# Keys of two MLA heads in one product, a new order at the change of layers and at the start, and a wait for GpSimd, in a two-layer hybrid attention kernel

## The chip, the cores and the metric

One core of one Trainium2 chip runs the whole program. The metric is the device time of one execution in microseconds; lower is better. "Span" is the time between the first and the last instruction that the profiler saw.

## The reference

Two layers over 256 context tokens and 512 latent tokens of width 1024, in float32. Each layer modulates a layer norm with shift and scale from `w_ada`, projects to 2784 columns and attends in three head groups. Only the MLA group is shown: its keys and values come from one product with `w_ukv`, in which each head has 64 key columns followed by 64 value columns.

```python
def mla_kv(zckv, zkr, g, w_ukv, tabs):
    kv = (rms_norm(zckv, g) @ w_ukv).reshape(B, L, MLA_HEADS, MLA_NOPE + MLA_V)
    k_nope, v = jnp.split(kv, [MLA_NOPE], axis=-1)
    ...
def hybrid_layer(...):
    sh_l, sc_l, gt_l = jnp.split(jax.nn.silu(c) @ p["w_ada"] + p["b_ada"], 3, axis=-1)
    hl = layer_norm(xl) * (1 + sc_l[:, None, :]) + sh_l[:, None, :]
    ... = jnp.split(hl @ p["w_in"], IN_SPLITS, axis=-1)
    ...
    y_l = merge_groups(o_a, o_b, o_m, ga_l, gb_l, gc_l, p["w_out"])
    xl_new = layer_norm(DEEPNORM_ALPHA * xl + gt_l[:, None, :] * y_l, p["ln_g"], p["ln_b"])
```

## The kernel before

Tokens lie in six tiles of 128 (tiles 0 and 1 are context, 2 to 5 latent). Every large product is done as three products on values split in a high and a low part (`three`, lines 982 to 984); ScalarE writes the high part of a weight slice (line 1515), GpSimd the low part (line 1899). The engines' programs are written out by hand, each in its own order, and meet only in semaphores; the SyncE queue issues all loads in its own order. So an instruction that waits holds all that is behind it on its engine.

Start (layer 0). Loads: tiles 0 to 3 of the input, the shift part of quarter 0 of `w_ada` (1 MB), tiles 4 and 5, its scale part, then weight pieces and quarters in turn. VectorE takes row statistics (`rows_in`), GpSimd the root, VectorE or ScalarE scales the rows (`scale_rows`), TensorE turns each tile (`turn_x`, line 1043), ScalarE copies it back (`put_back`). TensorE forms a quarter's modulation rows (`ada_half`, line 1009), VectorE copies them, TensorE turns and adds strips by a product with `pick` (`turn_quarter`, line 1024), VectorE adds the bias (`quarter_columns`), ScalarE modulates, VectorE splits, and `project` begins. Quarters 1 to 3 are turned between products of the first chunk.

Attention. 20 units in ten pairs per layer; units 14 to 19 are the six MLA heads, pairs 7 to 9. Pair p's scores, exponents (ScalarE, line 1627), partial sums (GpSimd, `sum_probs`, line 1954; last one VectorE, `sum_last`, line 2218) and value products overlap with the row maxima of the pairs behind it (`max_tile` on TensorE, line 1225; `reduce_max` on VectorE, line 2183). Products go through a ring of three PSUM banks in the order of the list `RING`. In pairs 4, 5 and 6 `mla_head` (line 1177) makes q and k of the units of the pair three further on: the even unit before scores 4, the odd one after scores 5. `mla_copy` takes them out of the ring on ScalarE, `mla_rope` turns q on VectorE, and a pair later `mla_high` (ScalarE) and `mla_low` (VectorE) split them. Today one "k" part has 128 stationary columns of one head, of which `mla_copy` keeps rows 0 to 63. Eight probability buffers are used in turn, so an exponent waits for the sums that read its buffer.

Change of layers. `project_out` ends with the second half of the output product, one tile after another in the order 2, 3, 4, 5, 0, 1 ("tile n" below and in the prediction counts in this order, from 0). Per tile VectorE does `gained_tile` (residual, centring, gain) and `new_row`; ScalarE squares twice (`square_rows`, line 1768), GpSimd takes roots (`row_root`), ScalarE writes the normalised row (`next_row`, line 1777), TensorE turns it, ScalarE modulates (`modulate_next`, line 1791), VectorE splits it (`split_next`, lines 2392 and 2393), and TensorE starts layer 1's first chunk with the slices that are ready: three of the ring (`NW`) and three held aside (`HELD`, slices 3 to 5) in buffers that the output product still reads, so that they are split at its end. Line 336 and line 274:

```python
def mla_parts(L):
    return [("q", 1), ("k", 1)] + ([("q", 0)] if L < DEPTH - 1 else []) + [("k", 0)]
HELD = [("in", 1, CHUNK_ORDER[0], k) for k in (3, 4, 5)]
```

## Time and profile before

| | us |
|---|---|
| median of 3 runs (lowest, highest) | 968.3 (966.56, 972.94) |
| the profiled execution | 967.27 |
| its span | 965.5 |
| TensorE busy | 923.2 |
| VectorE / GpSimd / ScalarE busy | 565.5 / 511.2 / 430.2 |

Busy times are unions of the instructions of an engine over the span. PE is TensorE, PEld its weight loads, DVE VectorE, ACT ScalarE, POOL GpSimd, SPq the SyncE queue. The start of the next product, not the duration of one, tells what a product costs, since they overlap in the pipeline. The granted clock is 1.00 at 2.4 GHz and 0.50 at 1.2 GHz.

### The profile page before, as it was taken

The page shows a single profiled execution, that of the slowest core. Times are in us where ns is not written, and L with a number is a line of the kernel's source. Part 1 is how long each engine was busy: PE and PEld are TensorE (multiplying, and loading weights), DVE is VectorE, ACT ScalarE, POOL GpSimd, SP SyncE. Part 2 cuts the span into 40 slices and gives each one's busy share as a digit, 9 for nine tenths or more (in the row PEclk, how much of TensorE's full clock was granted, in tenths as well). Part 3 has the DMA queues.
Part 4 walks back from the last instruction along what each step waited for, and adds up shares of the span by engine and source line. Part 5 has one row for each costly group of instructions (what it writes and reads, how often), then busy time and mean ns, then how long its engine had stood idle before and what let it go on. Part 6 is the DMA issues. An engine that isn't in the chain of part 4 may idle for free.

```text
span 965.5 us, 13483 instructions
## 1 busy us (share of the span) xinstructions
PE 923.2 (96%) x4699; PEld 665.4 (69%) x4699; DVE 565.5 (59%) x900; ACT 430.2 (45%) x877; POOL 511.2 (53%) x431
## 2 busy tenths in 40 slices
PE   5999999999999999999999799999999999999996
PEld 4678667889655665665678589888984555565684
DVE  5469133513687669962228838667257757884346
ACT  5331221413565466655234852235344545664432
POOL 3137223324687645565546517455438875466672
PEclk9999999999999999999999999999999999999998
DMA  9957672214533200020453202322352311020252
GB/s 321 279 209 242 217 244 78 76 39 100 133 70 80 50 17 18 18 66 1 146 177 113 81 16 77 87 81 82 83 121 63 71 46 25 9 74 10 85 178 88
DMA packets 51754, 95.85 MB, mean 99 GB/s; under 512 B 9508, under 2 KB 24720, under 8 KB 50664
## 3 DMA queue, kind: packets, MB, share of 16 engines
q1 hardware_dynamic: 51688, 94.99, 32.4%
q8 instruction: 39, 0.64, 0.3%
q14 instruction: 27, 0.22, 0.1%
HBM read 71.32 MB, written 4.21 MB: 78 GB/s over the span
## 4 chain that ended last, share of the span: by engine, by line
PE 83%; DVE 9%; ACT 4%; POOL 2%; issue 2%; DMA 0%; POOLq 0%; SPq 0%; ACTq 0%; DVEq 0%
PE banks L982 15%; PE banks L984 14%; PE banks L983 14%; PE banks L1250 12%; PE banks L1272 11%; PE banks L1225 6%; PE banks L993 2%; PE banks L1291 2%; PE banks L1284 1%; DVE negmax L2183 1%; DVE area_b L2352 1%; PE banks L1123 1%; PE banks L1387 1%; DVE scr L2349 1%; ACT late_bias L1768 1%
## 5 line engine op out<-in xcount | busy, mean ns | idle before, releaser
L1899 POOL TENSOR_TENSOR w_split<-w_raw,w_split 128x512 fp32r<-128x512 f32 (+4 forms) x121 | 147.7, 1230 | 224.4 <-ACT w_split L1515 224.4
L982 PE MATMUL banks<-w_split,area_a 128*128 128x512 f32 (+3 forms) x606 | 230.5, 380 | 9.0 <-DVE area_a L2393 6.8
L984 PE MATMUL banks<-w_split,area_a 128*128 128x512 f32 (+3 forms) x606 | 223.0, 368 | 0.0
L983 PE MATMUL banks<-w_split,area_a 128*128 128x512 f32 (+3 forms) x606 | 222.4, 367 | 0.0
L2183 DVE TENSOR_REDUCE negmax<-banks 128x1 f32<-128x768 f32 x160 | 149.2, 952 | 80.1 <-PE banks L1225 79.7
L1515 ACT ACTIVATE w_split<-w_raw 128x512 fp32r<-128x512 f32 (+4 forms) x121 | 68.5, 580 | 192.2 <-PE banks L984 185.4
L1627 ACT ACTIVATE area_z<-banks 128x512 f32<-128x512 f32 x196 | 108.8, 598 | 80.0 <-PE banks L1250 76.6
L982 PEld LDWEIGHTS banks<-w_split,area_a 128*128 128x128 f32 x606 | 114.5, 189 | 41.0 <-issue 19.1
L1250 PE MATMUL banks<-area_a 97*128 97x512 f32 (+4 forms) x448 | 129.0, 399 | 4.4 <-ACT area_z L1627 3.1
L984 PEld LDWEIGHTS banks<-w_split,area_a 128*128 128x128 f32 x606 | 114.5, 189 | 16.7
L983 PEld LDWEIGHTS banks<-w_split,area_a 128*128 128x128 f32 x606 | 114.8, 189 | 12.8
L1250 PEld LDWEIGHTS banks<-area_a 97*128 97x128 f32 (+2 forms) x448 | 77.2, 190 | 57.3 <-issue 23.9
L1272 PE MATMUL banks<-area_z,vals 128*64 128x512 f32 x360 | 92.5, 618 | 0.0
L1954 POOL TENSOR_TENSOR area_b<-area_b,area_z 128x512 f32<-128x512 f32 x56 | 74.0, 1344 | 19.0 <-ACT area_z L1627 19.0
L1225 PE MATMUL banks<-area_a 96*128 96x384 f32 (+1 forms) x288 | 77.2, 357 | 5.2 <-DVE negmax L2183 3.7
L1225 PEld LDWEIGHTS banks<-area_a 96*128 96x128 f32 (+1 forms) x288 | 49.7, 191 | 31.9 <-issue 25.1
L1954 POOL TENSOR_TENSOR w_raw<-w_raw,area_z 128x512 f32<-128x512 f32 x38 | 49.2, 1322 | 6.4 <-ACT area_z L1627 6.4
L2156 DVE COPY area_b<-banks 128x512 f32<-128x512 f32 (+1 forms) x27 | 15.7, 583 | 61.9 <-PE banks L1123 61.9
L1935 POOL TENSOR_TENSOR area_g<-area_g,o_v 128x768 f32<-128x768 f32 (+3 forms) x20 | 26.4, 1319 | 47.4 <-DVE o_v L2244 31.6
L1272 PEld LDWEIGHTS banks<-area_z,vals 128*64 128x64 f32 x360 | 21.4, 138 | 34.0 <-issue 24.4
L1515 ACT ACTIVATE area_b<-banks 128x512 f32<-128x512 f32 (+4 forms) x66 | 31.9, 510 | 28.6 <-PE banks L984 25.4
L1627 ACT ACTIVATE late_bias<-banks 128x512 f32<-128x512 f32 x64 | 35.5, 596 | 18.1 <-PE banks L1250 15.2
(224 smaller groups left out, 1475.0 us busy)
## 6 DMA issues: line engine op xcount, KB each, us to landing
w_raw<-in_w_in_dram SPq DMA_DIRECT2D x32, 512.0 KB, 4.6
area_g<-in_w_ada_dram SPq DMA_DIRECT2D x13, 1024.0 KB, 6.3
area_g<-in_w_ada_dram SPq DMA_DIRECT2D x16, 512.0 KB, 4.8
w_raw<-in_w_out_dram SPq DMA_DIRECT2D x16, 512.0 KB, 4.5
area_a<-parts SPq DMA_DIRECT2D x72, 96.0 KB, 2.2
area_a<-parts SPq DMA_DIRECT2D x30, 192.0 KB, 3.6
area_b<-in_x_dram SPq DMA_DIRECT2D x8, 512.0 KB, 7.4
w_raw<-in_w_in_dram SPq DMA_DIRECT2D x8, 352.0 KB, 3.3
```

The costliest lines, as they stand in the source:

```text
L982: nc.tensor.matmul(dst, a[0], b[0], start=first, stop=False)
L983: nc.tensor.matmul(dst, a[0], b[1], start=False, stop=False)
L984: return nc.tensor.matmul(dst, a[1], b[0], start=False, stop=last)
L1225: mm = nc.tensor.matmul(banks[:, b0 + j, 0:384], f[0][0:rows, t * P:(t + 1) * P], f[2][0:rows, j * 384:(j + 1) * 384], start=True, stop=True)
L1250: mm = nc.tensor.matmul(dst[:, at:at + cols.stop - cols.start], f[kf][0:rows, kt * P:(kt + 1) * P], f[qf][0:rows, cols], start=(i == 0), s ...
L1272: mm = nc.tensor.matmul(banks[64 * u:64 * u + 64, 3, :], vals[:, step, value_head(2 * p + u), :], prob(L, p, step, u), start=(step == 0), ...
L1515: return nc.scalar.activation(dst, src, ACT.Copy)
L1627: nc.scalar.activation(prob(L, p, step, u), banks[:, r % NRING, :], ACT.Exp, scale=SCALE[pair_family(p)]).then_inc(p_ready, 1)
L1899: op = nc.gpsimd.tensor_tensor(lo, raw, hi.bitcast(F32), ALU.subtract)
L1935: nc.gpsimd.tensor_tensor(g, g, o, ALU.mult).then_inc(gated, 1)
L1954: nc.gpsimd.tensor_tensor(total(L, p, u), first, prob(L, p, step, u), ALU.add).then_inc(pool_summed, 1)
L2183: nc.vector.tensor_reduce(negmax[:, p % 2, at:at + 1], banks[:, b0:b0 + 2, 0:384], AX.XY, ALU.max, negate=True).then_inc(max_read, 1)
```

## The change

MLA keys: an even unit has only its "q" parts; an odd unit's "k" parts use 128 stationary columns that hold the keys of both heads of the pair, and `mla_copy` copies rows 0 to 63 to the even unit's buffer and 64 to 127 to the odd one's. For that the split `ukv` is laid out with all keys first and all values behind. Change of layers: two slices are held (3 and 4), in `ukv` and in the free end of `parts`, which are free after the last scores; ScalarE and GpSimd split them around the first tile; slice 5 goes through the ring. The orders of ScalarE and VectorE for the last tiles are rewritten. GpSimd waits at the first sums of pair 1 for VectorE's last sums of pair 0. Start: tile 4 is loaded ahead of quarter 0; TensorE's and VectorE's orders are changed; a quarter is turned with four transposes, and VectorE sums the strips. Hunks that only pass the unit to `mla_parts` are left out, and leading context with them.

```diff
@@ -271,7 +271,7 @@
-HELD = [("in", 1, CHUNK_ORDER[0], k) for k in (3, 4, 5)]
+HELD = [("in", 1, CHUNK_ORDER[0], k) for k in (3, 4)]
@@ -333,9 +333,12 @@
-def mla_parts(L):
-
-    return [("q", 1), ("k", 1)] + ([("q", 0)] if L < DEPTH - 1 else []) + [("k", 0)]
+def mla_parts(L, u):
+
+    groups = (1, 0) if L < DEPTH - 1 else (1,)
+    if u % 2 == 0:
+        return [("q", g) for g in groups]
+    return [("q", 1), ("k", 1)] + [("q", g) for g in groups[1:]] + [("k", 0)]
@@ -376,13 +379,13 @@
-            RING += [("mla", _L, 2 * _p + 6, part) for part in mla_parts(_L)]
+            RING += [("mla", _L, 2 * _p + 6, part) for part in mla_parts(_L, 2 * _p + 6)]
         if now:
             RING += [("s", _L, _p, s, u) for s in (4, 5) for u in range(2)]
         if not last:
             RING += [("rows", _L, 1)]
         if head_pair(_p + 3):
-            RING += [("mla", _L, 2 * _p + 7, part) for part in mla_parts(_L)]
+            RING += [("mla", _L, 2 * _p + 7, part) for part in mla_parts(_L, 2 * _p + 7)]
@@ -757,10 +760,9 @@
-            for t in range(4):
+            for t in range(5):
                 load_x(t)
             load_quarter(0, 0)
-            load_x(4)
@@ -931,6 +933,12 @@
+        def held_slice(k):
+
+            flat = (ukv if k == 3 else parts)[:].rearrange("p a n -> p (a n)")
+            at = 0 if k == 3 else 2048
+            return [flat[:, at + i * 512:at + (i + 1) * 512] for i in range(2)]
+
@@ -939,7 +947,7 @@
-                hi, lo = late_slice(k - 3)
+                hi, lo = held_slice(k)
@@ -947,7 +955,9 @@
-                return [(flat[:, 0:768], ukv[:, 0, :], ukv[:, 1, :])]
+                src = flat[:, 0:768].rearrange("p (h z n) -> p z h n", h=6, z=2)
+                hi, lo = (ukv[:, i, :].rearrange("p (z h n) -> p z h n", z=2, h=6) for i in range(2))
+                return [(src[:, z], hi[:, z], lo[:, z]) for z in range(2)]
@@ -962,13 +972,13 @@
-                eng.wait_ge(filled, USE["y", s[1] - 1, 1, out_tiles(s[1] - 1)[-1]] + 1)
+                scored(eng, s[1] - 1, NPAIR - 1)
             elif s[0] in ("in", "out"):
                 slice_used(eng, s)
             if s[0] == "uq":
                 eng.wait_ge(filled, USE["z", s[1], LAST, TILES - 1] + 1)
             if s[0] == "out" and s[2] == 0 and s[3] < NW:
-                eng.wait_ge(ring_filled, N_RINGB["mla", s[1], NUNIT - 1, mla_parts(s[1])[-1]])
+                eng.wait_ge(ring_filled, N_RINGB["mla", s[1], NUNIT - 1, mla_parts(s[1], NUNIT - 1)[-1]])
@@ -1018,11 +1028,8 @@
-                for i in range(2):
-                    for w in range(2):
-                        at = w * 256 + i * P
-                        mm = nc.tensor.matmul(banks[:, 6, 4 * i + 2 * w:4 * i + 2 * w + 2], ada_rows[:, q % 2, at:at + P],
-                                              pick[:], start=True, stop=True)
+                for b in range(4):
+                    mm = nc.tensor.transpose(banks[:, 6, b * P:(b + 1) * P], ada_rows[:, q % 2, b * P:(b + 1) * P], ident[:])
@@ -1138,7 +1145,7 @@
-                v = [ukv[:, i, :].rearrange("p (h n) -> p h n", h=6)[:, :, 64:128] for i in range(2)]
+                v = [ukv[:, i, 384:768] for i in range(2)]
@@ -1186,7 +1193,7 @@
-                        mm = three(dst, [ukv[:, i, h * P:(h + 1) * P] for i in range(2)],
+                        mm = three(dst, [ukv[:, i, (h - 1) * 64:(h + 1) * 64] for i in range(2)],
@@ -1494,12 +1501,13 @@
-                    for t in range(4):
+                    for t in range(3):
                         turn_x(L, t)
                     ada_half(0, 0)
+                    turn_x(L, 3)
                     turn_x(L, 4)
+                    ada_half(0, 1)
                     turn_x(L, 5)
-                    ada_half(0, 1)
@@ -1579,17 +1587,23 @@
-                for part in mla_parts(L):
+                for part in mla_parts(L, u):
                     r = N_RINGB["mla", L, u, part] - 1
                     what, g = part
-                    rows = P if what == "q" else 64
+                    src = banks[:, r % NRING, 0:len(GROUPS[g]) * P]
                     act.wait_ge(ring_filled, r + 1)
-                    copy(qk_t[0:rows, 2 * (m % 2) + (what == "k"), tokens(g)],
-                         banks[0:rows, r % NRING, 0:len(GROUPS[g]) * P]).then_inc(ring_free, 1)
+                    if what == "q":
+                        op = copy(qk_t[:, 2 * (m % 2), tokens(g)], src)
+                    else:
+                        copy(qk_t[0:64, 2 * ((m - 1) % 2) + 1, tokens(g)], src[0:64])
+                        op = copy(qk_t[0:64, 2 * (m % 2) + 1, tokens(g)], src[64:128])
+                    op.then_inc(ring_free, 1)
             def mla_high(L, u):
                 m = N_MLA[L, u]
                 act.wait_ge(mla_roped, m)
+                if u % 2 == 0:
+                    act.wait_ge(ring_free, N_RING_FREE["mla", L, u + 1, mla_parts(L, u + 1)[-1]])
@@ -1815,23 +1829,24 @@
+                split_w(HELD[0])
                 square_rows("new", L, ts[0])
-                for n in range(1, len(ts)):
+                split_w(HELD[1])
+                for n in range(1, len(ts) - 1):
                     square_rows("next", L, ts[n - 1])
-                    if n == len(ts) - 1:
-                        for s in HELD:
-                            split_w(s)
                     square_rows("new", L, ts[n])
-                    if n == len(ts) - 1:
-                        next_row(L, ts[n - 1])
                     if n >= 3:
                         modulate_next(L + 1, ts[n - 3])
-                    if n < len(ts) - 1:
-                        next_row(L, ts[n - 1])
-                square_rows("next", L, ts[-1])
-                next_row(L, ts[-1])
-                for t in ts[-LAG:]:
-                    modulate_next(L + 1, t)
+                    next_row(L, ts[n - 1])
+                square_rows("next", L, ts[4])
+                modulate_next(L + 1, ts[2])
+                square_rows("new", L, ts[5])
+                next_row(L, ts[4])
+                modulate_next(L + 1, ts[3])
+                square_rows("next", L, ts[5])
+                modulate_next(L + 1, ts[4])
+                next_row(L, ts[5])
+                modulate_next(L + 1, ts[5])
@@ -1945,6 +1960,7 @@
+                        pool.wait_ge(dve_summed, N_DVE_SUM[L, 0, 1])
@@ -2035,11 +2051,10 @@
-                        if n == len(ts) - 1:
+                        row_root("new", L, ts[n])
+                        if n == 0:
                             split_w(HELD[0])
                             split_w(HELD[1])
-                        row_root("new", L, ts[n])
-                    split_w(HELD[2])
@@ -2406,11 +2421,15 @@
+                    if n == 5:
+                        split_next(ts[1])
                     gained_tile(n, t)
-                    if n > LAG:
-                        split_next(ts[n - LAG - 1])
+                    if n == 4:
+                        split_next(ts[0])
+                    elif n == 5:
+                        split_next(ts[2])
                     new_row(n, t)
-                for t in ts[-LAG - 1:]:
+                for t in ts[3:]:
@@ -2433,11 +2452,12 @@
-                col = ada_col[:, 0].rearrange("p (w k) s -> p k w s", w=2)[:, 2 * q:2 * q + 2]
-                sums = banks[:, 6, 0:8].rearrange("p (k w s) -> p k w s", k=2, w=2)
-                bias = bias_col[:].rearrange("p (w k) -> p k w", w=2)[:, 2 * q:2 * q + 2]
-                nc.vector.tensor_tensor(col, sums, bias.unsqueeze(3).broadcast_to((P, 2, 2, 2)),
-                                        ALU.add).then_inc(quarter_ready, 1)
+                strips = banks[:, 6, :].rearrange("p (b j r) -> p b r j", b=4, j=4)[:, :, 0:2, :]
+                chain(nc.vector.tensor_reduce(strip_sum[:], strips, AX.X, ALU.add))
+                col = ada_col[:, 0].rearrange("p (w k) s -> p w k s", w=2)[:, :, 2 * q:2 * q + 2]
+                bias = bias_col[:].rearrange("p (w k) -> p w k", w=2)[:, :, 2 * q:2 * q + 2]
+                nc.vector.tensor_tensor(col, strip_sum[:].rearrange("p (w k) s -> p w k s", w=2),
+                                        bias.unsqueeze(3).broadcast_to((P, 2, 2, 2)), ALU.add).then_inc(quarter_ready, 1)
@@ -2472,14 +2492,12 @@
-                    dve.wait_ge(pool_const, 1)
-                    nc.vector.tensor_reduce(pick[:], ident[:].rearrange("p (j r) -> p r j", j=4)[:, 0:2, :], AX.X, ALU.add)
                     rows_in(1)
                     rows_in(2)
                     scale_rows(1)
                     rows_in(3)
+                    rows_in(4)
                     scale_rows(3)
-                    rows_in(4)
```

## Rows read from the trace of the kernel before

**Rows 1.** The page: busy time, share of the span and instructions of TensorE
```profile
PE 923.2 (96%) x4699; PEld 665.4 (69%) x4699; DVE 565.5 (59%) x900; ACT 430.2 (45%) x877; POOL 511.2 (53%) x431
```

**Rows 2.** Waits of TensorE in the whole span: line, releaser, total, times, longest
```profile
PE banks L982 <- DVE area_a L2393: 6.8, 1, 6.8
...
PE banks L1291 <- DVE w_raw L2218: 1.0, 2, 0.7
```

**Rows 3.** Timeline, layer 1, pairs 5 and 6: start, duration, instruction, [idle before]
```profile
820.31 0.40 PE L982 MATMUL banks<-cmp_t,ukv 128*128 128x512 f32 x1
...
821.01 0.28 PE L982 MATMUL banks<-cmp_t,ukv 128*128 128x256 f32 x1
...
821.36 0.99 PE L1250 MATMUL banks<-area_a 97*128 97x512 f32 x2
...
822.74 1.82 DVE L2183 TENSOR_REDUCE negmax<-banks 128x1 f32<-128x768 f32 x2 [2.29 <-PE banks L1225]
...
828.99 1.08 ACT L1627 ACTIVATE area_z<-banks 128x512 f32<-128x512 f32 x2 [2.48 <-PE banks L1250]
```

**Rows 4.** Stretch of layer 0's pair 6: busy us of PE, PEld, DVE, ACT, POOL; clock
```profile
381.00:404.00 23.00, 22.47 (x115) 14.57 (x116) 21.02 (x26) 13.86 (x39) 14.72 (x11) 1.00 0.08 18
```

**Rows 5.** Line 1515 (ScalarE copies) from 330 to 420: ns min/median/max, forms
```profile
L1515 ACT ACTIVATE area_b<-banks x24: 378/490/601, 339.4 to 397.2; 128x512 f32<-128x512 f32 x6, 64x512 f32<-64x512 f32 x6, 128x256 f32<-128x256 f32 x6, 64x256 f32<-64x256 f32 x6
```

**Rows 6.** Timelines of VectorE, ScalarE, GpSimd and TensorE, change of layers
```profile
542.91 1.23 DVE L2393 TENSOR_TENSOR area_a<-area_z,area_a 128x1024 fp32r<-128x1024 f32 x1
...
546.65 0.69 DVE L2349 TENSOR_TENSOR scr<-banks,area_g 128x512 f32<-128x512 f32 x1
...
548.37 1.28 DVE L2373 SCALAR_TENSOR_TENSOR o_t<-area_b,row_mean,area_g 128x1024 f32<-128x1024 f32 x1
...
551.51 2.17 DVE L2393 TENSOR_TENSOR area_a<-area_z,area_a 128x1024 fp32r<-128x1024 f32 x1
...
542.82 2.88 ACT L1791 ACTIVATE area_z<-banks,ada_col 128x128 f32<-128x128 f32 x8
...
546.70 1.17 ACT L1768 ACTIVATE late_bias<-area_b,row_mean 128x1024 f32<-128x1024 f32 x1
...
549.66 2.94 POOL L1899 TENSOR_TENSOR cmp_t<-w_raw,cmp_t 128x512 fp32r<-128x512 f32 x2
...
553.73 0.79 PE L982 MATMUL banks<-w_split,area_a 128*128 128x512 f32 x1 [6.81 <-DVE area_a L2393]
```

**Rows 7.** Stretches with the granted clock (after the five busy times)
```profile
554.00:556.00 2.00, 2.00 (x5) 1.55 (x6) 1.60 (x1) 0.57 (x2) 1.61 (x2) 0.50 0.00 0
...
558.00:560.00 2.00, 2.00 (x12) 1.86 (x11) 0.88 (x1) 0.30 (x3) 1.42 (x3) 0.77 0.08 28
...
28.00:32.00 4.00, 4.00 (x38) 1.90 (x38) 0.90 (x2) 0.40 (x1) 1.27 (x1) 0.77 1.10 349
```

**Rows 8.** Timeline of the start
```profile
6.18 1.86 SPq L743 DMA_DIRECT2D area_g<-in_w_ada_dram  x1
...
14.80 1.28 DVE L2059 BATCH_NORM_STATS2 stats<-area_b 128x6 f32<-128x512 f32 x2
...
20.56 1.17 ACT L1515 ACTIVATE w_split<-w_raw 128x512 fp32r<-128x512 f32 x2
...
20.75 1.07 PE L1009 MATMUL banks<-area_g,c_silu 128*32 128x256 f32 x16
...
23.99 2.51 ACT L1544 ACTIVATE area_b<-area_b,ada_col 128x256 f32<-128x256 f32 x4 [1.29 <-DVE ada_col L2439]
```

**Rows 9.** DMA issues from 6 to 6.5: KB each, us to landing
```profile
area_g<-in_w_ada_dram SPq DMA_DIRECT2D x1, 1024.0 KB, 12.8
```

**Rows 10.** Timeline: a quarter turned today (x8) and four plain transposes (x4)
```profile
33.31 0.95 PE L1024 MATMUL banks<-pick,o_t 128*128 128x2 f32 x8
...
294.09 0.60 PE L1302 MATMUL banks<-ident,scr 128*128 128x128 f32 x4
```

**Rows 11.** Timeline, layer 1: VectorE's last sums of pair 0
```profile
734.95 4.23 DVE L2218 TENSOR_TENSOR w_raw<-w_raw,late_bias 128x512 f32<-128x512 f32 x2
```

More of the change, by code:

```diff
@@ L460, in hybrid_layers @@
         bias_col = sb("bias_col", [P, 16])
-        pick = sb("pick", [P, 2])
+        strip_sum = sb("strip_sum", [P, 4, 2])
         stats = sb("stats", [P, TILES, 2, 6])
@@ L642, in operands_free @@
             elif u == 19:
-                eng.wait_ge(ring_filled, N_RINGB["mla", L, 19, mla_parts(L)[-1]])
+                eng.wait_ge(ring_filled, N_RINGB["mla", L, 19, mla_parts(L, 19)[-1]])
             else:
@@ L1581, in mla_copy @@
                     act.wait_ge(split_lo, N_SPLIT[L, "gqa2"])
-                for part in mla_parts(L):
+                for part in mla_parts(L, u):
                     r = N_RINGB["mla", L, u, part] - 1
                     what, g = part
-                    rows = P if what == "q" else 64
+                    src = banks[:, r % NRING, 0:len(GROUPS[g]) * P]
                     act.wait_ge(ring_filled, r + 1)
-                    copy(qk_t[0:rows, 2 * (m % 2) + (what == "k"), tokens(g)],
-                         banks[0:rows, r % NRING, 0:len(GROUPS[g]) * P]).then_inc(ring_free, 1)
+                    if what == "q":
[4 more added lines that the diff above has]
+                    op.then_inc(ring_free, 1)
             def mla_high(L, u):
```

2 lines of the change are left out of this document (1 added, 1 removed).

## The prediction

> **What bounds the kernel now.** I read four views in this order. The page first: TensorE is busy for 923.2 us of a span of 965.5 [rows 1], and no other engine comes near, so time falls only where TensorE gets less to do or stands less. The reader is to see how little standing there is to win: 42 us in all. The waits of TensorE say where [rows 2]: one wait of 6.8 us for VectorE's split of a tile (line 2393, the change of layers) is by far the longest, and two for the last sums (line 2218) make 1.0 us. Then the timeline around the edited places, and the granted clock of the stretches: after the long wait TensorE runs at half rate for some 5 us [rows 7]. The profiled execution took 967.27 us (span 965.5 and 1.8 around it); the median of the runs shown is 968.3, 1.0 above. I make the sum on 967.27 and add that 1.0 at the end.
>
> **Keys of two heads in one product.** Today `mla_head` uses 128 stationary columns of one head, 64 key columns and 64 value columns that `mla_copy` throws away. Afterwards two heads' keys fill the 128, on odd units only; for units 14, 16, 18 in each layer the two "k" parts vanish. One pair of parts is three products of 512 columns and three of 256: 820.31 to 821.36, that is 1.05 us [rows 3]. Six units: 6.3 us of pure TensorE work. Is it on the path? Behind the even unit's products, VectorE stood 2.29 us at 822.74 until TensorE's next maximum tile [rows 3]; so there the saving goes straight through. Against it: in one of the four pairs in which VectorE also splits MLA operands (`mla_low`; p = 5 and 6 of both layers) it is busy 21.02 of 23.00 us [rows 4], TensorE 22.47. The 1.98 us that VectorE has free exceed 1.05, but not all lie in the right place. I take 1.05 in the two pairs p = 4 and 0.85 in the other four: 2.1 + 3.4 = **5.5**; bounds 2.1 (nothing in the four) and 6.3. ScalarE's copies stay equal in number but move: an odd unit has two more, 0.60 and about 0.38 us, since 64 and 128 rows cost the same [rows 5]. Queued behind them is the next pair's first exponent, before which ScalarE stands 2.48 us today [rows 3]: hidden, at most 0. What they cost if that cover goes is the last rival. The even unit's rope waits only for "q" now, earlier than before; `mla_high` of the even unit waits for copies that ScalarE has already done in its own order. The `ukv` split in two instructions each on ScalarE and GpSimd adds a start-up or two where both idle: 0. The ring has two slots fewer at an even unit; the slots then needed (the row maxima, the outputs) are freed long before: 0.
>
> **Change of layers.** (Tiles are counted here in the order in which the output product makes them, 0 to 5.) Today TensorE starts tile 1 at 553.73, 6.81 us after the end of tile 0's products [rows 6]. VectorE first does `gained_tile` for tile 5 (from 546.65 until the instruction begun at 548.37 ends at 549.65), then the split of tile 1, whose second half takes 2.17 us instead of the 1.23 of tile 0's, because GpSimd splits held slices from 549.66 [rows 6]. The new order: the split of tile 1 stands ahead of `gained_tile` of tile 5; its input is ready (ScalarE modulates it from 542.82 for 2.88 us [rows 6]). So it runs 546.65 to about 548.6 without GpSimd beside it (some 0.7 for the copy and 1.23). The held slices are split some 25 us earlier, in a buffer free since the last scores; what they delay is VectorE's chain for tile 0, which is serial from there on and never waits for TensorE. I charge 1.0, one VectorE instruction lengthened as above (2.17 - 1.23 = 0.94); bounds 0 and 1.9 (two). Tile 1 is thus ready at 549.6 and TensorE waits 2.9 us. What is late next: turning tile 5 needs `next_row`(5), which stands on ScalarE behind the square of tile 5 and the modulation of tile 4. Walking the lists with 1.2 for a square (546.70 [rows 6]) and as much for a row, 2.9 for a modulation and 1.9 for a split gives 562.6 for it, while TensorE arrives 2.5 us sooner. Two waits, 5.4 us. Today's loss is 6.8 plus the low clock: 0.50 granted in 554 to 556 and 0.77 in 558 to 560 [rows 7], so low until about 558.9, 5.2 us at half rate, 2.6 lost; 9.4. Difference 4.0. A clock that falls in the first wait is mostly absorbed by the second; I keep 0.5 for it: **3.5**, bounds 0 (both waits with a full low stretch, and VectorE delayed by 1.9) and 6. Slice 5, no longer held, goes into the slot of slice 0, free when the last tile has used it: 12 products of 0.23 us (820.31 to 821.01 for three [rows 3]) are 2.8 us of cover for one ScalarE and one GpSimd split (0.6, and 1.5 as in the 2.94 for two [rows 6]): 0. Its piece stays longer in the raw buffer, and the SyncE queue waits there before a load wanted tens of us later: 0.
>
> **The lock between VectorE and GpSimd.** The row shows 0.94 us for one VectorE instruction beside GpSimd's split [rows 6]. The Trainium skill, "SBUF — State Buffer", Who interferes with whom, says more: whoever comes first holds the shared ports for its whole instruction and the other is fully blocked. By that rule two GpSimd splits of 1.47 us each (2.94 for two [rows 6]) could cost the chain 2.9 instead of my 1.0, and the sum would be 1.9 us smaller. It speaks against the early split; the last sums below show a blocking of that size, so I keep it in the range.
>
> **Start.** The tile-4 row statistics begin at 14.80 [rows 8] because tile 4's load is queued behind the first 1 MB of weights; moved ahead of it they follow tile 3's at about 13.3. Tile 5's load keeps its place, behind the same bytes. The second half of quarter 0 is issued at 6.18 [rows 8] and lands 12.8 us later [rows 9], at 19.0, yet its products start at 20.75 behind tile 5's transposes [rows 8]; queued only behind tile 4's they start at about 19.1. The turned quarter is then there near 22.0. ScalarE, however, still has to split two slices (until 21.7 [rows 8]) and to copy tile 5 back, 2 x 0.6, until about 22.8; `modulate`(0) started at 23.99 [rows 8]: 1.2 gained, and TensorE's first product follows it. The other three quarters are turned while TensorE never waits: eight passes of 0.95 us become four of 0.60 [rows 10], 0.35 x 3 = 1.05. VectorE's extra sum (some 0.2 us on 128x32) lies in the slack while TensorE works on the slice before. Together **2.2**, bounds 0.5 and 3.5.
>
> **GpSimd waits.** The wait holds the first sums of pair 1 until VectorE's two last sums of pair 0 are done; queued behind are GpSimd's sums of pair 1 and its gate, and for them ScalarE's exponents eight buffers later. In layer 1 the two sums took 4.23 us [rows 11], where one instruction of that shape alone takes 0.69 (546.65 [rows 6]), and TensorE waited for such sums 0.7 and 0.3 us [rows 2]. The wait removes that; GpSimd starts about 1.3 us later in each layer and has idle time to catch up. **0.8**, bounds -1.0 and 1.5.
>
> **Sum.** 5.5 + 3.5 + 2.2 + 0.8 = 12.0; 967.27 - 12.0 = 955.3; plus 1.0 gives 956.3.
>
> **The rivals.** (1) VectorE takes over in the four busy pairs: their 3.4 us come to nothing, 959.7. For it: rows 4; against it: its stand of 2.29 us. (2) The change of layers gives nothing: two waits and low clock after each cost what one did, 956.3 + 3.5 = 959.8. For it: half rate [rows 7] followed the wait of 6.8 us; against it: the first wait shrinks by more than half. (3) The start stays at the low clock for longer: in 28 to 32 it was 0.77 [rows 7]; all of it at 0.50 would lose 1.1 more, 957.4. The Trainium skill, "TensorE: Matmul & The Clock Gate", PE-mode transpose, would have it so: transposes do not count as activity as products do, and here they replace products in the turns. (4) Slower: the bunched copies of an odd unit hold the next exponents, the probabilities come late, TensorE stands 1.0 us at the head of each next pair and the clock falls as after the long wait, 2.6 lost each time. It decides once ScalarE's 2.48 us in front of that exponent [rows 3] are used up. Six times 3.6 is 21.6: 956.3 + 21.6 = 977.9, slower than before.
>
> **How the numbers follow.** Forecast 0.62, rivals (1) 0.13, (2) 0.12, (3) 0.08, (4) 0.05. The time is the likeliest's, 956.3. Its own terms at their better ends make 950.7, at their worse ends 966; both at once is unlikely, so the range is 951.5 to 963.5. A measurement of this kernel tells about 1% from no change, 9.7 us; that is 958.6. Forecast and (3) lie below it but for their tails, (1) and (2) just above: faster 0.67, within 0.29, slower 0.04.
>
> **What would show it.** Right: 18 fewer products of each of 512 and 256 columns reading `ukv` in `mla_head`; TensorE's busy time down by about 7 us; at the change of layers two waits of 2 to 3 us, for VectorE's split and then for ScalarE's row, in place of one of 6.8; the first product near 24.3 instead of 25.5; sums at line 2218 of 0.7 us each. Wrong: new idle time of TensorE before scores of pairs 5 to 7, or a third low-clock stretch.

## The result, and the profile after

| | before | changed |
|---|---|---|
| median of the timed runs (lowest, highest), us | 967.43 (965.15, 972.94) | 954.94 (953.89, 955.12) |
| ratio to before, 95% interval | | 0.9862 (0.9833 to 0.9890) |
| span of the profiled execution, us | 965.5 | 953.1 |

The forecast was 956.3 us in a range of 951.5 to 963.5; the change is faster by 12.5 us, 1.3%. The same kernel measured twice more, beside later runs of the kernel before, gave ratios of 0.9852 and 0.9836.

The page of the changed kernel, its span and the line that answers to [rows 1]:

```profile
span 953.1 us, 13390 instructions
...
PE 912.2 (96%) x4647; PEld 654.0 (69%) x4647; DVE 563.3 (59%) x903; ACT 430.1 (45%) x879; POOL 512.7 (54%) x433
```

TensorE has 11.0 us less of busy time. The span fell by 12.4, so nearly all of it is work or low-clock time that is gone, and only 1.4 is standing. The prediction had put the busy time at about 7 less: it counted the products left out, but busy time also shrinks where products that ran at half clock now run at full clock, and the mean granted clock of the span went from 0.987 to 0.994.

The waits of TensorE in the changed kernel (line, releaser, total, times, longest), which answer to [rows 2]; line 992 was 982, line 2408 was 2393:

```profile
PE banks L1232 <- DVE negmax L2198: 4.2, 11, 0.8
PE banks L992 <- issue: 3.7, 2, 3.0
...
PE banks L992 <- DVE area_a L2408: 2.1, 1, 2.1
...
PE banks L1050 <- ACT vals L1791: 1.3, 1, 1.3
```

The reader is to see that the wait of 6.8 us is now one of 2.1 and one of 1.3, and that the wait for VectorE's last sums is no longer in the list. Of the two "issue" waits the longer, 3.0, stands in front of the first product, the other, 0.7, at the change of layers.

To see where the time went I cut each span at five instructions that both kernels have: the first product that forms the gate rows of layer 0 (512 columns with `c_silu`, line 993 before and 1003 changed; it comes some 46 us behind the first product of `project`), the first tile turned for layer 1, the last value product of layer 1 that reads `ukv`, the first turned row maximum of layer 1, and the last value product of the attention. Lengths in us, from the timelines ("full" and "half": whether the clock granted from the first product of `project` on was 1.00 or had a stretch at 0.50):

| kernel | start | layer 0 | change of layers | to the maxima | attention, layer 1 | rest |
|---|---|---|---|---|---|---|
| before | 71.9 (half) | 459.2 | 140.7 | 42.9 | 192.6 | 58.2 |
| changed | 70.1 (half) | 457.0 | 136.9 | 43.6 | 187.2 | 58.3 |
| changed, f1 | 67.2 (full) | 456.7 | 136.8 | 43.7 | 187.3 | 58.2 |
| e1, old keys | 67.8 (full) | 458.8 | 136.7 | 43.0 | 189.8 | 58.3 |
| e2, old change of layers | 67.6 (full) | 456.8 | 140.8 | 43.1 | 187.9 | 58.3 |
| e3, old start | 71.7 (half) | 456.7 | 136.7 | 42.9 | 188.0 | 58.3 |
| f2, keys alone | 73.0 (half) | 457.1 | 140.1 | 43.0 | 187.8 | 58.2 |
| f3, split behind | 67.2 (full) | 456.8 | 141.0 | 43.3 | 187.2 | 58.3 |
| g2, no wait | 70.6 (half) | 458.3 | 136.4 | 43.6 | 187.8 | 58.3 |
| g3, wait alone | 72.8 (half) | 458.5 | 141.1 | 42.9 | 191.4 | 58.3 |

The four profiles that the table leaves out start with 67.0 (e4, full), 67.3 (g1, full), 69.1 (f4, half) and 70.3 (g4, half).

Between the first two rows: start 1.8, layer 0 2.2, change of layers 3.8, attention of layer 1 5.4, and 0.7 given back ahead of it. No term of the forecast has that 0.7. Most of it is a wait that the kernel before does not have there, for a transfer into `area_a`, ahead of a product of the first maxima:

```profile
690.48 0.58 PE L1232 MATMUL banks<-area_a 96*128 96x384 f32 x2 [0.43 <-DMA area_a<-ones_r]
```

Three other profiles with the new order have it too (f1 0.49, f4 0.50, g2 0.43), the rest don't; why is open. Each stretch below is priced by the rows in which only one part differs.

### The profile page after: what moved, and what is told of

Read it like the earlier page. It is cut to its first block, busy times and chain, and to the rows that moved or that the text cites. A ratio compares the mean times of both kernels' runs of the same rounds, so it can differ in the third digit from the quotient of the medians.

```text
span 953.1 us, 13390 instructions
## 1 busy us (share of the span) xinstructions
PE 912.2 (96%) x4647; PEld 654.0 (69%) x4647; DVE 563.3 (59%) x903; ACT 430.1 (45%) x879; POOL 512.7 (54%) x433
## 4 chain that ended last, share of the span: by engine, by line
PE 78%; DVE 9%; ACT 6%; POOL 2%; issue 2%; DMA 1%; SPq 1%; POOLq 0%; ACTq 0%; DVEq 0%
PE banks L992 14%; PE banks L994 13%; PE banks L993 13%; PE banks L1257 12%; PE banks L1279 10%; PE banks L1232 6%; ACT area_z L1805 2%; DVE negmax L2198 2%; PE banks L1003 2%; PE banks L1298 1%; PE banks L1291 1%; ACT late_bias L1782 1%; DVE area_b L2367 1%; PE banks L1130 1%; PE banks L1394 1%
## 5 line engine op out<-in xcount | busy, mean ns | idle before, releaser
L1641 ACT ACTIVATE area_z<-banks 128x512 f32<-128x512 f32 x196 | 108.4, 599 | 72.8 <-PE banks L1257 69.9
```

The source lines that it names most:

```text
L1641: nc.scalar.activation(prob(L, p, step, u), banks[:, r % NRING, :], ACT.Exp, scale=SCALE[pair_family(p)]).then_inc(p_ready, 1)
```

## The experiments

Twelve runs in three sets, each set on one chip beside runs of the kernel before. The first four undo one part of the change each. Their set has no run of the changed kernel, so they are held against its first measurement (ratio 0.9833 to 0.9890), and the intervals of all four overlap that: what tells these four apart from it is their traces.

**Old keys.** `mla_parts`, the layout of the split `ukv`, `mla_high` and `mla_copy` as before.

```diff
-    if u % 2 == 0:
-        return [("q", g) for g in groups]
-    return [("q", 1), ("k", 1)] + [("q", g) for g in groups[1:]] + [("k", 0)]
+    return [("q", 1), ("k", 1)] + ([("q", 0)] if L < DEPTH - 1 else []) + [("k", 0)]
```

> The changed kernel with one head's keys per product again, the rest as changed. Theory A (the products left out lie on the path): the layer-0 part of the lead goes back by about 2.5 us and the layer-1 part by 3 to 4, in all 5.5 to 6.5 us slower than the changed kernel's 954.9, so about 961 us and a ratio to the kernel before of about 0.993. Theory B (VectorE's pairs take the saving, and layer 1's lead comes from the low-clock stretch that is gone): 2 to 3 us slower, about 957.5.

Measured: 958.43 us, ratio 0.9895 (0.9865 to 0.9925), so 3.3 thousandths of 968 us, 3.2 us, above the first measurement of the changed kernel. The distances between the turned row maxima price it better. The three pairs with MLA work take 26.20, 24.94 and 26.61 us in layer 0 against 25.15, 24.72 and 25.95 in the changed kernel (1.05, 0.22, 0.66), and 22.51, 21.78 and 23.07 in layer 1 against 21.31, 21.11 and 22.35 (1.20, 0.67, 0.72): 4.5 in all, between the two theories. Timeline of TensorE, layer 0, in the pair that saved 0.22; first with the old keys, then changed (start, duration, instruction, [idle before]):

```profile
360.80 0.40 PE L987 MATMUL banks<-cmp_t,ukv 128*128 128x512 f32 x1
...
362.21 0.28 PE L987 MATMUL banks<-cmp_t,ukv 128*128 128x256 f32 x1
...
363.54 0.65 PE L1252 MATMUL banks<-area_a 97*128 97x512 f32 x2
364.03 0.52 PE L1227 MATMUL banks<-area_a 96*128 96x384 f32 x2
```

```profile
362.63 0.69 PE L1257 MATMUL banks<-area_a 97*128 97x512 f32 x2
363.16 0.52 PE L1232 MATMUL banks<-area_a 96*128 96x384 f32 x2
363.52 0.74 PE L1257 MATMUL banks<-area_a 97*128 97x512 f32 x2
364.75 0.59 PE L1232 MATMUL banks<-area_a 96*128 96x384 f32 x2 [0.49 <-DVE negmax L2198]
```

In the changed kernel the products that read `ukv` are gone from the even unit, and TensorE stands 0.49 us for VectorE's maximum shortly behind, where it did not stand with the old keys. So VectorE takes part of the saving in this pair. In the other three busy pairs no new wait of this kind is in the timeline: there single products of scores and maxima start some tenths later than they did with the old keys (in layer 0's last such pair one maximum product starts 0.64 us behind the product ahead of it, where it was 0.33), and what holds them is not shown.

**Old change of layers.** Three held slices and the old orders of ScalarE, VectorE and GpSimd there.

```diff
-HELD = [("in", 1, CHUNK_ORDER[0], k) for k in (3, 4)]
+HELD = [("in", 1, CHUNK_ORDER[0], k) for k in (3, 4, 5)]
...
-                    if n == 5:
-                        split_next(ts[1])
                     gained_tile(n, t)
-                    if n == 4:
-                        split_next(ts[0])
-                    elif n == 5:
-                        split_next(ts[2])
+                    if n > LAG:
+                        split_next(ts[n - LAG - 1])
```

> The changed kernel with the old order at the change of layers and three slices held late. Theory A: the wait of 6.8 us at tile 1 and the low clock behind it come back, 3.7 us slower than 954.9, about 958.6. Theory B (what is won there is lost again while layer 1 starts): at most 1 us slower, about 955.5.

Measured: 957.20 us, ratio 0.9883 (0.9856 to 0.9911). Its change of layers takes 140.8 us again. Its longest wait for VectorE, and its windows (busy us of PE, PEld, DVE, ACT, POOL; granted clock; DMA):

```profile
PE banks L986 <- DVE area_a L2402: 7.2, 1, 7.2
```

```profile
544.00:548.00 4.00, 0.60 (x2) 0.51 (x3) 3.31 (x2) 4.00 (x11) 3.83 (x5) 0.63 0.36 90
548.00:552.00 4.00, 4.00 (x13) 3.12 (x12) 3.83 (x5) 1.47 (x3) 1.36 (x3) 0.52 0.34 90
552.00:556.00 4.00, 4.00 (x23) 3.37 (x21) 0.54 (x1) 2.48 (x5) 1.32 (x3) 1.00 0.00 0
```

The long wait is back, and the half clock with it, as in [rows 7].

**Old start.** Tile 4 behind quarter 0, the old orders, the quarters turned with `pick`.

```diff
-            for t in range(5):
+            for t in range(4):
                 load_x(t)
             load_quarter(0, 0)
+            load_x(4)
...
-                    ada_half(0, 1)
                     turn_x(L, 5)
+                    ada_half(0, 1)
```

> The changed kernel with the old start, quarters turned by the product with pick. Theory A: 1.8 to 2.2 us slower than 954.9, about 957; the first product at 25.5 instead of 23.9 us and each turn 0.35 us longer. Theory B (transposes keep the clock low, so the earlier start is worth only what the low clock takes): less than 1 us slower.

Measured: 957.07 us, ratio 0.9878 (0.9852 to 0.9905). The first product comes at 25.25 us, where it came at 23.91 in the changed kernel and at 25.48 in the kernel before; the start takes 71.7 us.

**Without the wait of GpSimd.**

```diff
-                        pool.wait_ge(dve_summed, N_DVE_SUM[L, 0, 1])
```

> The changed kernel without GpSimd's wait for the last sums. Theory A (the sums of VectorE and GpSimd block one another): two sums at the start of layer 1's pair 1 take over 4 us again and TensorE waits 0.7 us for them, 0.5 to 1.0 us slower than 954.9. Theory B (TensorE's wait was hidden elsewhere): no change within 0.3 us. Theory C (a wait more there tips the clock): 2 us or more slower.

Measured: 958.34 us, ratio 0.9882 (0.9848 to 0.9917), but with a profiled execution of only 952.14 and timed ones from 955.3 to 961.33: wider than any other kernel of the set. The third set has it again. In its profile the two sums of layer 1 take 2.61 us and TensorE does not wait for them, so theory A's 4 us and its wait of 0.7 did not come back.

The second set takes the largest single term apart, and does the keys alone.

**The changed kernel again.** No edit; the measure for this set.

> The changed kernel itself, for the others of this set and for how far its executions differ. Theory A: its first products run at full clock in some executions and at half clock in others (the profiled one had half clock from 23 to 30 us), so profiled spans lie 2 to 3 us apart for the same code, with all stretches behind 40 us equal to 0.2 us. Theory B: the low clock belongs to the change (transposes in place of products) and comes every time: the stretch from the start to the first product of the gates is 70.1 us again.

Measured: 953.47 us, ratio 0.9852 (0.9818 to 0.9885). Its span is 949.9, 3.2 shorter than that of the first profile, 2.9 of it in the start. The two windows of the start, of the first profile of the changed kernel and of this one (they stand 2.96 and 2.46 us in front of the first product):

```profile
24.00:28.00 4.00, 4.00 (x9) 2.72 (x9) 2.54 (x6) 1.55 (x3) 0.75 (x1) 0.50 1.08 361
28.00:32.00 4.00, 4.00 (x39) 2.23 (x39) 0.69 (x1) 0.00 (x0) 0.52 (x1) 0.78 1.10 350
```

```profile
24.00:28.00 4.00, 4.00 (x42) 2.40 (x42) 2.36 (x6) 1.03 (x2) 0.04 (x1) 1.00 1.10 364
28.00:32.00 4.00, 4.00 (x20) 3.31 (x21) 1.28 (x4) 0.86 (x2) 1.25 (x1) 1.00 1.08 348
```

One program, two clocks: after a similar stand the first products get 1.2 GHz in one execution and 2.4 GHz in another.

**Keys alone.** The kernel before with the key part only (the changed kernel with the other three parts undone as above).

> The kernel before with the keys of two heads in one product and nothing else of the change. Expected from the distances between the row maxima of successive pairs in the earlier run without this part: 1.9 us in layer 0 and 2.6 in layer 1, 4.5 in all (the forecast had 5.5), ratio to the kernel before 0.995. Rival: the key part only pays with the rest in place (the low clock of layer 1 stays), under 2.5 us; or it pays its full 6.3 us.

Measured: 962.84 us, ratio 0.9954 (0.9926 to 0.9983): 4.5 us of 967.82. That is the sum of the distances under the old keys, found the other way round.

**The split of tile 1 behind `gained_tile`.** All else as changed, the early held splits too. It asks whether the gain at the change of layers comes from GpSimd's early splits or from VectorE's order.

```diff
-                    if n == 5:
-                        split_next(ts[1])
                     gained_tile(n, t)
+                    if n == 5:
+                        split_next(ts[1])
```

> The changed kernel with VectorE's split of tile 1 behind its work on tile 5 again; the slices still held early. Theory A (the place in VectorE's order is what was won): TensorE waits 2.1 + 3.0 us at tile 1, low clock behind it, at least 2 us slower than the changed kernel in the stretch between the first turned tile and the last value product. Theory B (early holding, so no GpSimd split beside VectorE, is what was won): within 0.7 us of the changed kernel.

Measured: 958.15 us, ratio 0.9903 (0.9869 to 0.9937), 4.7 above the changed kernel of its set; the shortest of its six times, 955.85, is above the longest of the changed kernel's, 954.77. The row and the window:

```profile
545.88 0.79 PE L992 MATMUL banks<-w_split,area_a 128*128 128x512 f32 x1 [5.14 <-DVE area_a L2408]
```

```profile
546.00:550.00 4.00, 4.00 (x10) 3.02 (x11) 3.10 (x5) 1.19 (x2) 1.86 (x2) 0.50 0.00 0
```

TensorE stands 5.14 us and then runs at half clock; the change of layers takes 141.0, as in the kernel before. Without these two lines the whole of that gain is gone; the early splits and the rest of the new order alone bring none. Whether the two lines would bring it with the slices split late was not run.

**TensorE turns tile 5 late.** The products of all five slices for tile 0 come first, and tile 5 is turned behind the last slice of tile 3. An attempt at a better kernel: more work in front of the two waits that are left.

```diff
+                    pe.wait_ge(w_lo, N_SLICE["in", L, c_, begun - 1])
+                    pe.wait_ge(next_ready, N_NEXT[L, order[0]])
+                    for k in range(begun):
+                        product(k, order[0])
                     for ks in (range(NW), range(NW, begun)):
...
-                        for t in order[:LAG - 1]:
+                        for t in order[1:LAG - 1]:
...
-                            if n == 0 and k == 0:
+                            if n == 0 and k == begun - 1:
                                 turn_x(L, order[LAG + 2])
```

> The changed kernel with TensorE doing all five slices of tile 0 before tile 1 and turning tile 5 behind all five slices of tile 3. Theory A (TensorE waits for ScalarE's row of tile 5 while products of tile 3 are ready): the second wait of 2.0 us goes, a wait of up to 1.4 us for tile 5's split comes, 0.6 to 1.2 us faster than the changed kernel. Theory B (ScalarE's chain sets the end of the stretch in any order): within 0.3 us.

Measured: 954.95 us, ratio 0.9870 (0.9838 to 0.9903), against 953.47 and 0.9852 of the changed kernel in its set: no gain. The waits only moved (timeline of TensorE; the last two stand ahead of products of 256 columns):

```profile
540.67 0.47 PE L992 MATMUL banks<-w_split,area_a 128*128 128x512 f32 x1 [0.72 <-issue]
...
545.09 0.50 PE L992 MATMUL banks<-w_split,area_a 128*128 128x512 f32 x1 [0.77 <-DVE area_a L2411]
...
554.33 0.50 PE L992 MATMUL banks<-w_split,area_a 128*128 128x512 f32 x1 [0.31 <-DVE area_a L2411]
...
560.22 0.36 PE L992 MATMUL banks<-w_split,area_a 128*128 128x256 f32 x1 [1.31 <-ACT area_z L1808]
...
563.51 0.39 PE L992 MATMUL banks<-w_split,area_a 128*128 128x256 f32 x1 [1.26 <-DVE area_a L2411]
```

Their sum is 4.4 us against 4.2 in the changed kernel, and the change of layers takes 137.3 against 136.8. That fits theory B, in which the chain of ScalarE and VectorE through the six tiles sets the end of the stretch now; other orders of TensorE were not run.

The third set asks about the wait of GpSimd, in both directions, and about the turned quarters.

**The changed kernel, a third time.**

> The changed kernel once more, beside the same kernel without GpSimd's wait. Expected 953 to 955 us, its executions within 4 us of one another; the profiled span 949.9 or 953.1, by the clock of the first products alone.

Measured: 952.95 us, ratio 0.9836 (0.9809 to 0.9864).

**Without the wait, again.** Same edit as above.

> The changed kernel without GpSimd's wait, again: the first time its profiled span was 950.0 but its median 958.3 with executions from 952.1 to 961.3. Theory A (the wait is worth the 0.5 us that the two profiles show in layer 1, the rest was the low clock's chance at the start): median within 1.5 us of the changed kernel's in this set. Theory B (without the wait the clock falls in layer 1 in many executions): median 3 us or more slower again, and a stretch below 1.00 in layer 1's attention if the profiled execution is such a one.

Measured: 960.16 us, ratio 0.9900 (0.9870 to 0.9930). Its interval and that of the changed kernel in this set don't touch: 6.4 thousandths, 6.2 us. Theory B's two signs are there, the slower median and a stretch below 1.00 in layer 1 (0.72 in 728 to 732), but the traces show far less than 6.2 us (below).

**The wait alone**, in the kernel before.

```diff
+                        pool.wait_ge(dve_summed, N_DVE_SUM[L, 0, 1])
```

> The kernel before with GpSimd's wait and nothing else. Theory A (VectorE and GpSimd block one another there): the pair of layer 1 that took 15.34 us between its row maxima takes 13.9 to 14.5, 0.5 to 1.5 us off the span, ratio about 0.999. Theory B (it also keeps the clock up in layer 1): pair distances 16 and 17 lose the 1.5 us of the low stretch as well, up to 3 us off.

Measured: 966.49 us, ratio 0.9974 (0.9955 to 0.9993), 1.9 us faster than before by the medians, 2.5 by the ratio. In layer 1 the pair in question takes 13.84 us from one turned maximum to the next, 13.84 to 13.87 in the three profiles of the changed kernel, 14.47 and 14.50 in the two without the wait, and 15.34 in the kernel before. But keys alone (f2), which has no wait either, takes 14.50, so 0.84 of the 1.50 between before and this run is there without the wait.

**Quarters turned with `pick`**, the rest of the start as changed.

```diff
-                for b in range(4):
-                    mm = nc.tensor.transpose(banks[:, 6, b * P:(b + 1) * P], ada_rows[:, q % 2, b * P:(b + 1) * P], ident[:])
+                for i in range(2):
+                    for w in range(2):
+                        at = w * 256 + i * P
+                        mm = nc.tensor.matmul(banks[:, 6, 4 * i + 2 * w:4 * i + 2 * w + 2], ada_rows[:, q % 2, at:at + P],
+                                              pick[:], start=True, stop=True)
```

> The changed kernel with quarters turned and summed by the product with pick, all other orders of the start as changed. Theory A: each turn takes 0.4 us longer, the three in the first chunk 1.1 to 1.2 us, the first adds 0.2 to 0.4 at the start: 1.3 us slower at equal clock (first product of the gates at 68.5 instead of 67.2 with full clock). Theory B (transposes let the clock fall at the start, products don't): the low stretch never comes here and the median is no slower than the changed kernel's.

Measured: 954.64 us, ratio 0.9850 (0.9822 to 0.9877): 1.4 thousandths above the changed kernel of its set, 1.4 us, inside the uncertainty. The price of one turn is in the timelines of TensorE, from its start to that of the next product, with `pick` and (the second fence, the f1 profile) with transposes:

```profile
31.77 0.95 PE L1034 MATMUL banks<-pick,o_t 128*128 128x2 f32 x8
32.57 0.49 PE L992 MATMUL banks<-w_split,area_a 128*128 128x512 f32 x1
```

```profile
30.07 0.60 PE L1032 MATMUL banks<-ident,o_t 128*128 128x128 f32 x4
30.43 0.47 PE L992 MATMUL banks<-w_split,area_a 128*128 128x512 f32 x1
```

0.80 against 0.36, so 0.44 for each of the three turns that TensorE does without standing.

## Why the prediction was right, step by step

**Keys, 5.5 said, 4.5 measured.** The count came out: 36 products that read `ukv` with 128 rows of `cmp_t` where there were 72, that is 18 fewer of 512 columns and 18 of 256. The price of 1.05 per pair held in full in the two pairs p = 4 (1.05 and 1.20). The term that was mis-sized is the 0.85 for each of the four busy pairs: 0.22, 0.66, 0.67 and 0.72, so 2.3 for 3.4. In the pair that saved 0.22, VectorE's free 1.98 us lay in the wrong place in part, as the prediction feared, and the wait of 0.49 shows it; in the other three the cause is open. Rival (1), nothing in these pairs, is refuted; of the 4.2 us that four times 1.05 would be, 1.9 were lost, where 0.8 had been charged. Rival (4) too: the exponent that had 2.48 us of cover in [rows 3] still has 1.35 in the changed kernel, and none of the six pairs got longer.

**Change of layers, 3.5 said, 3.8 measured.** (Between the profiles; 4.0 between e2 and the profiles of the changed kernel.) The steps, on the timeline of the changed kernel:

```profile
516.89 2.23 DVE L2394 SCALAR_TENSOR_TENSOR area_b<-o_t,row_std,area_g 128x1024 f32<-128x1024 f32 x1 [0.81 <-POOL row_std L1934]
...
523.47 1.28 DVE L2394 SCALAR_TENSOR_TENSOR area_b<-o_t,row_std,area_g 128x1024 f32<-128x1024 f32 x1 [1.06 <-POOL row_std L1934]
...
540.23 1.23 DVE L2408 TENSOR_TENSOR area_a<-area_z,area_a 128x1024 fp32r<-128x1024 f32 x1
...
543.96 0.69 DVE L2407 CAST area_a<-area_z 128x1024 fp32r<-128x1024 f32 x1
...
544.69 1.23 DVE L2408 TENSOR_TENSOR area_a<-area_z,area_a 128x1024 fp32r<-128x1024 f32 x1
...
516.75 1.29 POOL L1914 TENSOR_TENSOR ukv<-w_raw,ukv 128x512 fp32r<-128x512 f32 x1
518.00 2.29 POOL L1914 TENSOR_TENSOR parts<-w_raw,parts 128x512 fp32r<-128x512 f32 x1
...
541.56 0.47 PE L992 MATMUL banks<-w_split,area_a 128*128 128x512 f32 x1 [0.74 <-issue]
...
545.97 0.51 PE L992 MATMUL banks<-w_split,area_a 128*128 128x512 f32 x1 [2.09 <-DVE area_a L2408]
...
558.25 1.09 PE L1050 MATMUL banks<-ident,vals 128*128 128x128 f32 x8 [1.34 <-ACT vals L1791]
```

The second half of tile 1's split takes 1.23 us where it took 2.17 [rows 6]. The prediction priced that half alone; in the kernel before the first half, the cast, was long too, beside the same splits of GpSimd:

```profile
549.68 1.79 DVE L2392 CAST area_a<-area_z 128x1024 fp32r<-128x1024 f32 x1
```

It takes 0.69 now, so VectorE spends 2.0 us less on the split, not 0.94. GpSimd's two early splits made one VectorE instruction 2.23 long instead of 1.28, 0.95 for the 1.0 that was charged. The two waits were put at 2.9 and 2.5 and are 2.09 and 1.34. A third, of 0.74 in front of tile 0, was not forecast: the view puts it down to "issue", but it ends 0.10 us after the second half of tile 0's split does (540.23 and 1.23), which is where a later chain of VectorE shows. Together 4.2 for 5.4. Rival (2) is refuted by e2. That a low clock after the first wait would be absorbed by the second was a reason given for keeping the cost small, and two other profiles let it be seen: e3 was granted 0.57 in 548 to 552 and g4 0.81 and 0.77 in 544 to 552, the changed kernel 1.00, and all three take 136.7 to 136.9 for the stretch; the second wait, 1.34 in the changed kernel, is in neither of the two. A full wait followed by no second one, as in e2 and f3, is not so forgiven.

The Trainium skill, "SBUF — State Buffer", Who interferes with whom, has whoever comes first hold the shared ports for a whole instruction; the prediction made of it that VectorE could be held up by both splits, and the sum for this part 1.9 smaller. The rows agree with the rule and not with what was made of it: GpSimd's first split had begun 0.14 us earlier and ended at 518.04, and VectorE's instruction was 0.95 longer; then GpSimd's second split took 2.29 instead of 1.29. They took turns, so VectorE paid for one split, not for two.

**Start, 2.2 said, 1.8 or 4.7 measured.** The first product came at 23.91 for a forecast of 24.3, and between 23.52 and 24.37 in the ten profiles of the new order, so this step held; a turn gives 0.44 for 0.35. What the sum lacked is the clock. All four profiles of the old order had a stretch at half clock behind the start's stand (71.7 to 73.0 us); of the ten with the new order six ran at full clock (67.0 to 67.8) and four had such a stretch (69.1 to 70.6). Whether the order or chance decides it, four profiles and ten don't show. Against the 71.9 of before, the profile compared at first gives 1.8, and f1 gives 4.7. Rival (3), a start longer at low clock, came true in the profile compared: 20 to 24, 24 to 28 and 28 to 32 were granted 0.87, 0.50 and 0.78 in the changed kernel where before had 1.00, 0.81 and 0.77, and that ate part of the gain. It is not what the new order brings, since six of its ten profiles had no low clock there at all. That the first profile gave 1.8, near the 2.2, is luck in part. The Trainium skill, "TensorE: Matmul & The Clock Gate", PE-mode transpose, says that transposes do not count as busy in the same way. g4, with products instead, had 0.57 in 24 to 28; f1 and g1, with transposes, had 1.00. The runs do not bear a cost of that kind out here, and the first transposes of the changed kernel speak against it:

```profile
9.38 3.69 PE L1050 MATMUL banks<-ident,area_b 128*128 128x128 f32 x16 [5.85 <-ACT area_b L1535]
13.29 1.09 PE L1050 MATMUL banks<-ident,area_b 128*128 128x128 f32 x8 [0.22 <-ACT area_b L1535]
14.31 1.07 PE L1019 MATMUL banks<-area_g,c_silu 128*32 128x256 f32 x16
```

Within the first sixteen they start 0.21 us apart, the eight behind start 0.11 apart: the clock doubled while TensorE, after standing 5.85 us, had done nothing but transposes.

**GpSimd's wait, 0.8 said, its mechanism shown in layer 0 only.** The sums in the timelines of VectorE, layer 1: the changed kernel, then g2 without the wait.

```profile
727.43 2.15 DVE L2233 TENSOR_TENSOR w_raw<-w_raw,late_bias 128x512 f32<-128x512 f32 x2
```

```profile
729.32 2.64 DVE L2232 TENSOR_TENSOR w_raw<-w_raw,late_bias 128x512 f32<-128x512 f32 x2
```

TensorE's wait of 0.7 for them is gone, but it isn't there in e4, f2 and g2 either, which have no wait of GpSimd: in layer 1 only the profile of before had it. In layer 0 TensorE waited 0.31 or 0.32 us for such sums in three of the four profiles without GpSimd's wait (before, f2, g2; not e4) and in none with it. "0.7 each" was wrong, 2.15 for two, since another GpSimd instruction (line 1975, from 727.14 for 1.28) still lies beside the first. Undisturbed, in e2, the two took 1.30. By the distances between turned maxima the wait gives 0.63 in this pair (14.47 to 13.84), 0.26 in the next (16.41 to 16.15) and takes 0.41 in the third (16.97 to 17.38), 0.5 together, and 0.0 to 0.5 in layer 0: 0.5 to 1.0, the size predicted. That the wait itself gives the 0.63 is not shown (see the last section). The timed runs say more: by the ratios 2.5 us alone, and undone 1.9 (against the first measurement of the changed kernel) and 6.2. The profile of g2 is 5.4 longer than that of g1; 3.3 lie in the start and are its clock, 1.8 in layer 0, and attention gives 0.5. Of the 1.8, 0.5 is the pair of the wait, and 1.2 lie behind the last turned maximum, where TensorE stands 0.72 us for GpSimd's split in `parts` (0.36 in the first profile of the changed kernel, no such wait in g1). What the remaining microseconds of the timed executions are is not shown by any trace and stays open.

**The sum.** 12.0 was forecast on the profiled execution and 12.4 came, by the spans. (The terms at their better and worse ends make 951.0 and 966.7, not the 950.7 and 966 written there; nothing hangs on it.) Two errors hid behind this. The keys gave 1.0 less. And the profile of before held low-clock stretches in the attention of layer 1 that no step had priced. The windows of the kernel before:

```profile
732.00:736.00 4.00, 3.80 (x12) 2.74 (x14) 3.70 (x5) 2.17 (x4) 4.00 (x4) 0.63 0.00 0
...
816.00:820.00 4.00, 4.00 (x13) 1.48 (x10) 4.00 (x4) 0.05 (x1) 4.00 (x3) 0.71 0.21 50
```

The second cost 1.46 us (23.24 for a pair that takes 21.78 in e1, which has the same keys and a full clock there). Its like came in 2 of the 13 other profiles (g3, 0.57 in 836 to 840, and f4, 0.75 in 824 to 828), one with the old keys and one with the new, so it isn't the keys that remove it. The changed kernel's profile had none: 1.5 us of its 12.4 are such a chance. The four parts alone come to about 11 (4.5, 3.8, 1.8 and 0.5 to 1.0), so that the whole met 12.0 within 0.4 is luck in part.

## What to carry to other kernels

Where a tuned kernel's engines run hand-written orders, look for the instruction that stands in front of the one the bounding engine waits for: here, without two moved lines on VectorE, everything else done at the same place was worth nothing. A saving of pure TensorE work need not pass to the time in full where another engine is nearly as busy (0.22 to 0.72 of 1.05 us here), so price it pair by pair and not from the free share of a stretch. And a stand of TensorE has a second price, the half clock that can follow it, which may or may not be paid in a given execution: before a difference of one or two microseconds is explained from one profile each, list the low-clock windows of both.

## What the runs showed of the hardware that was not expected

The clock behind the same stand differs between executions of one program. At the start (2.3 to 3.0 us of stand) the changed kernel got 0.50 once and 1.00 twice, and this alone moved its span by 3 us. Around the sums of layer 1, where TensorE stands three times for 0.3 to 0.8 us, all four profiles without GpSimd's wait had low windows (the lowest 0.63 to 0.73), and of the ten with it only e2 and e3 (0.74). The pair took 13.84 to 13.88 us where the clock stayed full. Where it was low it took 14.47 to 14.52, with the wait (e2, e3) as without it (e4, f2, g2), and 15.34 in before. So what goes with the wait in this pair is a clock that doesn't fall. But the wait is not shown to be its cause. In g2 TensorE keeps the starts it has in g1, counted from the first turned maximum of layer 1 and to 0.1 us, until the clock falls within 724 to 728, and the GpSimd instruction that the wait of this layer would hold back starts only at 729.68. What tips the clock, here and in e2 and e3, is open.

What VectorE and GpSimd cost each other isn't one number for one place. VectorE's two sums took 1.30 us undisturbed (e2), 2.64 in g2, where the two GpSimd instructions beside them took 3.42 instead of 2.52, and 4.23 in the kernel before [rows 11], where GpSimd's kept their 2.52. GpSimd's lines, first in g2, then in the kernel before:

```profile
729.68 3.42 POOL L1969 TENSOR_TENSOR w_raw<-area_z 128x512 f32<-128x512 f32 x2
```

```profile
735.51 2.52 POOL L1954 TENSOR_TENSOR w_raw<-area_z 128x512 f32<-128x512 f32 x2
```

In g2 they took turns, in the kernel before VectorE alone stood. The Trainium skill, "SBUF — State Buffer", Who interferes with whom, has issue order decide who blocks. By their starts in the traces VectorE's first sum is ahead of these in both, by 0.36 us in g2 (729.32) and by 0.56 in the kernel before (734.95), so issue order, as far as starts show it, does not tell the two outcomes apart. The prediction took the worse of them as the price that the wait removes, and of the four profiles without the wait only the one it was read from has it (4.23; 2.36, 2.61 and 2.64 in f2, e4 and g2).
